# Two constant products in each of TensorE's two later routing waits, in a four-layer transformer kernel on one Trainium2 core

## What is computed

```python
def hierarchical_moe(h, w_rg, b_rg, w_re, b_re, w_gate, w_up, w_down):
    xf = h.reshape(t, d)                                   # t = 256 tokens, d = 1024
    group_logits = xf @ w_rg + b_rg                        # 4 groups
    grp = argmax(group_logits); p_grp = softmax(group_logits)[grp]
    expert_logits = (xf @ w_re + b_re).reshape(t, 4, 8)    # 8 experts in each group
    top_logit, top_local = top_k(expert_logits[grp], 2)    # two experts for each token
    gates = p_grp * softmax(top_logit)
    experts = grp * 8 + top_local
    # the 512 (token, expert) pairs are sorted by expert, cut into blocks, and for each block
    y = (silu(xb @ w_gate[e]) * (xb @ w_up[e])) @ w_down[e]
    # every token adds its two results, each times its gate
```

## Time and profile before

| | |
|---|---|
| median of three runs | 1895.18 us (1894.8 to 1901.27) |
| span of the profiled execution | 1897.5 us |
| the mixture's jobs, first layer | from 857.9 us to about 1250 us of the span |
| the mixture's jobs, second layer | from 1440.3 us to about 1880 us |
| TensorE busy | 1822.5 us, 96% of the span |
| mean granted TensorE clock over the span | 0.987 |
| read from memory | 546.83 MB |

### The profile page before, as it was taken

One profiled execution on the slowest core, in us unless ns is written; L12 is line 12 of the kernel. 1 busy time (PEld: TensorE's weight loads), 2 busy tenths in 40 slices (PEclk: granted clock), 3 DMA queues, 4 the chain that ended last, 5 costly groups with the idle time before them and its releaser, 6 DMA issues.

```text
span 1897.5 us, 27293 instructions
## 1 busy us (share of the span) xinstructions
PE 1822.5 (96%) x10299; PEld 1179.9 (62%) x10299; DVE 861.8 (45%) x1611; ACT 765.6 (40%) x1392; POOL 105.0 (6%) x146
## 2 busy tenths in 40 slices
PE   8999999998999999999999999999999999999997
PEld 6779998886799988974334333335975333433334
DVE  4766656678765566873112111114784111211113
ACT  5554334556543335532333333334542333333333
POOL 3420000112100000010000000000010000000000
PEclk9999999998999999999999999999998999999999
DMA  9545555551355554449999999998557999999995
GB/s 318 201 161 185 193 179 177 166 180 55 110 189 179 181 184 149 162 195 374 419 427 427 427 429 428 429 428 336 186 211 276 411 427 428 427 428 426 428 428 217
DMA packets 130593, 549.40 MB, mean 290 GB/s; under 512 B 8030, under 2 KB 67768, under 8 KB 103480
## 3 DMA queue, kind: packets, MB, share of 16 engines
q1 hardware_dynamic: 127080, 539.53, 72.3%
q0 software_dynamic: 3088, 8.10, 1.3%
q10 hardware_dynamic: 320, 0.34, 0.1%
HBM read 546.83 MB, written 1.11 MB: 289 GB/s over the span
## 4 chain that ended last, share of the span: by engine, by line
PE 75%; DMA 17%; DVE 5%; ACT 1%; POOL 1%; issue 1%; SPq 0%; POOLq 0%; DVEq 0%; ACTq 0%
PE pb L1350 28%; DMA raw<-in_w_expert_down 16%; PE pb L1912 14%; PE pb L1941 11%; PE pb L1645 6%; PE pb L1920 2%; PE pb L1930 2%; PE pb L1479 1%; PE pb L1456 1%; PE pb L1502 1%; PE pb L1579 1%; DVE parts L2104 1%; POOL rms L893 1%; PE pb L1362 1%; PE pb L1858 1%
## 5 line engine op out<-in xcount | busy, mean ns | idle before, releaser
L2104 DVE TENSOR_TENSOR parts<-raw,parts 128x2048 fp32r<-128x2048 f32 (+1 forms) x138 | 307.2, 2232 | 109.3 <-ACT parts L913 106.3
L913 ACT ACTIVATE parts<-raw 128x2048 fp32r<-128x2048 f32 (+1 forms) x138 | 256.6, 1867 | 210.9 <-PE pb L1350 154.4
L1912 PE MATMUL pb<-raw,xw 128*64 128x512 f32 x1360 | 323.9, 608 | 10.9 <-DMA raw<-in_w_expert_gate 10.9
L1350 PE MATMUL pb<-xT,parts 128*128 128x256 f32 (+1 forms) x2712 | 333.3, 283 | 0.0
L1350 PEld LDWEIGHTS pb<-xT,parts 128*128 128x128 f32 (+1 forms) x2712 | 329.2, 191 | 4.7 <-issue 2.9
L2720 DVE TENSOR_TENSOR qk<-qk,pb 128x256 f32<-128x256 f32 x126 | 53.1, 422 | 550.0 <-ACT qk L1205 549.8
L1350 PE MATMUL pb<-parts,xT 128*128 128x512 f32 (+1 forms) x1200 | 273.4, 386 | 2.7 <-DVE xT L2115 1.5
L1350 PEld LDWEIGHTS pb<-parts,xT 128*128 128x128 f32 x1200 | 218.8, 190 | 49.2 <-issue 4.0
L1912 PEld LDWEIGHTS pb<-raw,xw 128*64 128x64 f32 x1360 | 87.5, 138 | 156.4 <-issue 133.3
L1941 PE MATMUL pb<-raw,qk 128*64 128x512 f32 x624 | 142.8, 596 | 20.3 <-DMA raw<-in_w_expert_down 20.2
L1200 ACT ACTIVATE qk<-pb 128x512 f32<-128x512 f32 x126 | 74.9, 595 | 195.4 <-PE pb L1912 195.4
(11 more groups left out here) (338 smaller groups left out, 1692.9 us busy)
## 6 DMA issues: line engine op xcount, KB each, us to landing
raw<-in_w_expert_gate SPq DMA_DIRECT2D x41, 2048.0 KB, 10.0
raw<-in_w_expert_up SPq DMA_DIRECT2D x37, 2048.0 KB, 10.4
raw<-in_w_expert_down SPq DMA_DIRECT2D x35, 2048.0 KB, 10.7
spare<-in_w_expert_down SPq DMA_DIRECT2D x16, 2048.0 KB, 15.1
spare<-in_w_expert_up SPq DMA_DIRECT2D x14, 2048.0 KB, 13.4
raw<-in_w_ffn_gate SPq DMA_DIRECT2D x22, 1024.0 KB, 5.2
raw<-in_w_ffn_up SPq DMA_DIRECT2D x22, 1024.0 KB, 5.1
raw<-in_w_ffn_down SPq DMA_DIRECT2D x22, 1024.0 KB, 4.9
```

What stands on the lines that cost most here:

```text
L913: nc.scalar.activation(parts[:, (SPL0[seg] + k) % SPL, 0, 0:kk * nn], raw[:, place, 0:kk * nn], ACT.Copy).then_inc(hi_done[seg], 1)
L1350: ins = mm(out_ap, b if flip else a, a if flip else b, start=first and n == 0, stop=last and n == 2)
L1912: ins = mm(pb[m][rows, :], xw[:, 4 * hf + k, :], w[:, k, :], start=(hf == 0 and k < 2), stop=(hf == 1 and k >= 2))
L2104: v.tensor_tensor(two[:, 1, :], raw[:, place, 0:kk * nn], two[:, 0, :].bitcast(F32), ALU.subtract)\
```

## The change

Two calls of `spin(2)` are put into TensorE's list in the routing, one behind L1841 and ahead of the wait for the job table's columns, the other behind L1845 and ahead of the wait for the first selection. That is two times four more passes in each of the two layers. Nothing else is changed.

```diff
                 mm(pb[3][0:1, JOBS:2 * JOBS], cst[0:1, C_I512 + W:C_I512 + W + 1], ij, start=True, stop=False).then_inc(pos_ready, 1)
+                spin(2)
                 pe.wait_ge(job_cols, l + 1)
                 ja, jo, jv = jobs_work()
                 mm(pb[3][0:1, JOBS:2 * JOBS], jv, jo, start=False, stop=True)
...
                 def tokens(i, t, k):
                     return xsp[:, i, D * t + P * k:D * t + P * (k + 1)]
 
+                spin(2)
                 for t in range(NT):
                     for i in range(2):
                         if i == 0:
```

## The result

| | median of its runs | ratio to before, 95% interval |
|---|---|---|
| before | 1896.59 us (7 runs, 1894.73 to 1901.27) | |
| changed | 1889.12 us (7 runs) | 0.9949 [0.9934, 0.9963] |
| predicted | 1884.8 us (range 1882.8 to 1891.5) | 0.9945 (1884.8/1895.18) |

The changed kernel is about 0.5% faster. It was timed on three further occasions, each with its own runs of the kernel before beside it: 0.9934, 0.9942 and 0.9945, medians 1885.71, 1887.46 and 1887.52 us. By the medians the gain was 7.5, 11.5, 9.5 and 9.8 us, and their plain quotients are 0.9961, 0.9940, 0.9950 and 0.9948, so 0.4 to 0.6%.

The account below looks back on a forecast made before the run. It took DMA to set each layer's end, with holes where loads wait for a half-clocked TensorE. 4.8 + 4.8 + 0.8 = 10.4 us off 1895.2 gave 1884.8 us, range 1882.8 to 1891.5 us.

Parts of the forecast that it names:

- the 3.3 us ahead of the fall: Routing stretch before the clock drops: TensorE busy 1.17 us, 2.9 us with both calls, like a stretch that kept its clock.
- The cost of the two calls: Routing waits: first call delays the table's product 0.05 us (bound 0.2), second delays the gather 0 (bound 0.1).
- The gain on TensorE: Gather and job 0 at full clock in place of half: L1874 starts 5.0 us earlier a layer.
- The short stop ahead of the last eight: In the gather, the last 8 of 32 products wait for VectorE's low parts until 853.66 us, costing nothing.
- DMA passes it on: In the expert jobs, weight loads follow the earlier TensorE, so 4.8 us a layer reaches the layer's end.
- rival 1: In the expert jobs, DMA returns only its idle time, not all its shortfall: 4.9 us, 1890.3 us; chance 0.28.
- DMA's holes: First layer's jobs, 860 to 890 us: DMA at 292 and 383 GB/s, 5.3 us lost, which an earlier TensorE fills.
- The dip at 930 us: First layer's jobs: DMA at 381 GB/s, 1.1 us lost; the load waits for TensorE and shifts with it.
- The 0.15 us that were taken off for DMA: Deduction a layer for what DMA can't follow around 930 us, estimated as a seventh of 1.1 us.
- The third term: Second layer's spin(8), starting earlier, may meet less half clock: 0.8 us taken, bounds 0 and 1.6 us.
- The forecast's own range: Whole kernel: 1883 to 1887 us if the forecast's mechanism holds, which had chance 0.56.
- The rule on idle gaps: Skill page's rule: only clearly longer TensorE gaps cost the clock, so filling these waits changes nothing, 1895.2 us.

Follow-up runs that it names:

- e2: Only the first `spin(2)`, ahead of the wait for the job table's columns, added to the kernel before: 1898.28 us, ratio 1.0001.
- e4: `spin(1)` in place of `spin(2)` at both places of the change: 1897.03 us, ratio 1.0000 to the kernel before.
- e7: `spin(4)` at both places, added to the kernel before: 1890.92 us, ratio 0.9959.
- e8: Changed kernel with its spin(8) split, four products ahead of the row products and four behind: 1889.69 us, ratio 0.9953 to the kernel before.
- e9: Changed kernel with the spin(8) split into two spin(4), plus spin(3) in the wait this opened: 1885.50 us, ratio 0.9940 to the kernel before.
- e3: Only the second `spin(2)`, ahead of the selection's wait, added to the kernel before: 1898.03 us, ratio 1.0003.
- e1: The changed kernel again, no edit, against the kernel before: 1885.71 us, ratio 0.9934.
- e5: The changed kernel once more, no edit, against the kernel before on another occasion: 1887.46 us, ratio 0.9942.
- e10: The changed kernel on a further occasion, no edit, against the kernel before: 1887.52 us, ratio 0.9945.
- e6: `spin(4)` at the second place alone, ahead of the selection's wait, added to the kernel before: 1893.76 us, ratio 0.9979.

## Why the prediction was right, point by point

**The clock is the cause, and both waits are needed.** Right as far as the change goes: the traces of its three repetitions hold 1.00 from L1824 through job 0 in both layers. The prediction argued from the busy time of the 3.3 us ahead of the fall. e2 to e4 show how weak that is as a measure: the clock fell in a stretch busy for 2.97 of 3.35 us. What they support is narrower: in these runs four products of 128x256 in the two waits kept the clock, two didn't, and four in the second wait alone did so in one layer of two. Why the clock falls where it does stays open; that its fall is what cost the time is shown, since the gather and job 0 hold the same products in all these kernels and took 14.0 to 16.2 us with the fall and 10.9 to 11.0 us without.

**The cost of the two calls.** Predicted 0.05 us and 0 of bounds 0.2 and 0.1; measured 0 for both, to 0.01 us. The margin is thin, as e7 shows: the next two products cost 0.84 us.

**The gain on TensorE, 5.0 us a layer.** Measured 4.73 us, in both layers. Two pieces are missing. Job 0 starts 3.88 us behind the gather and not 3.71. The products of the gather came 0.111 us apart and not 0.107, half of their spacing at half clock, so that VectorE's scaling, which needs the 28th, began 3.40 us behind the gather's start and not 3.2. The short stop ahead of the last eight did not show: L2573 ends at 855.92 us, and the 25th product starts at 856.00 us, 0.11 us behind the 24th like all others. And job 0 takes 7.02 us and not 6.85, up to L1876's start. Here the prediction's own figures don't agree: 5.3 us for 23.8 records is 0.223 us each, or 7.1 us for all 32, and not 0.213. The records do come 0.213 us apart, but the first and the last step take longer.

**DMA passes it on.** Right, and rival 1 is out: TensorE's 4.73 us are all there at the second layer's logits (553.21 us between before, and 553.08, 553.03 and 553.12 us in the three traces of the change), and DMA's holes are filled. It stayed full behind them and made up the hole, since it had lost more than TensorE gained. The dip at 930 us stayed, as predicted, because the load there waits for TensorE. The 0.15 us that were taken off for DMA were not needed. The time alone would not have shown this: 1889.12 us is nearer to rival 1's 1890.3 than to the forecast's 1884.8, and it is the traces that rule rival 1 out.

**The third term, 0.8 us.** The times can't tell it, and the traces speak for more than was taken. These are the lengths of the half clock, in us, at the places where the traces differ, beside e7's in the jobs. The spin(8) of e8 and e9 is split, so their columns for it mean the same stretch of the routing.

| trace | about 93 us | spin(8), first layer | gather, first layer | spin(8), second layer | gather, second layer |
|---|---|---|---|---|---|
| before, e2 | 3.4 | 3.4 | 10.2 | 6.8 | 10.2 |
| e3 | 3.4 | 3.4 | 10.2 | 6.8 | 13.6 |
| e4 | none | 6.8 | 6.8 | 6.8 | 10.2 |
| the change (e1, e5, e10), e7 | 6.8 | 6.8 | none | 3.4 | none |
| e6 | 6.8 | 6.8 | none | 3.4 | 10.2 |
| e8 | 3.4 | none | 13.6 | none | 13.6 |
| e9 | none | none | none | none | none |

The prediction said that the second layer's spin(8) may meet less half clock, because all is earlier there. In all five traces with the spin(8) whole in which the first layer's gather kept its clock it met 3.4 us, and in the four in which the clock fell there it met 6.8. That is 1.65 us, just beyond the bound of 1.6, where 0.8 was taken. The first layer's 6.8 us in place of 3.4 cannot be the change's, since they lie ahead of the first new product, and the column of 93 us differs already. In the spans they hide the gain in the second layer. These are single executions, so how often either happens is open. The runs of the change range over 6 us, those with a mean granted clock of 0.994 at 1884.1 to 1885.5 us and those with 0.991 at 1888.6 to 1890.5. All three profiled ones are of the second kind, so that no trace shows where the others had less half clock; it moves a run's time by as much as a layer's gain.

**The sum.** Twice 4.73 is 9.5 us, and 11.1 with the 1.65 us of the second layer, against 10.4. The four medians give 7.5 to 11.5 us, 9.6 on average, so they don't decide between these. From the 1896.6 to 1897.3 us of the kernel before on the four occasions 9.5 us lead to 1887.1 to 1887.8 us; measured were 1885.7 to 1889.1. Of the 4.3 us between the forecast and 1889.12, 1.4 us are the median of three runs that it started from, 1895.18 us, and 2.9 us the gain of 7.5 in place of 10.4. The forecast's own range, 1883 to 1887 us, holds one of the four medians; two lie 0.5 us above it and one 2.1 us. The wider range holds all four, but 1889.12 us lies in the part of it that was there for rival 1, which did not happen. So the mechanism was right, and that the range held this median was partly luck. The line of 0.5%, 9.5 us, is just where the gain lies, so that faster or the same was an even matter, and 0.44 to 0.53 was a fair price for it.

**The rule on idle gaps.** The Trainium skill, page "TensorE: Matmul & The Clock Gate", section "Why this matters for your kernels", warns of long idle gaps between bursts. The runs don't agree with it as a sufficient rule: in e4 the gaps were 0.38 and 0.50 us, and the clock fell. And filling waits of 1.01 and 1.12 us, which by that rule would change nothing, gave 4.73 us a layer.

## What to carry to other kernels

Look for stretches at 0.50 in the clock column and read what TensorE did ahead of them. Here it was short products of few rows or columns, with waits of about 1 us for another engine, and the bill was paid by the big products behind. Filler cost nothing here where its array time (0.85 us) was less than the wait (1.01 and 1.12 us), and it had to be enough: one call alone or one product in each wait gave nothing, four products in one wait gave a part, and twice the total cost 1.3 us a layer. When DMA bounds the stage behind, ask whether it had holes that were TensorE's. Here they were larger than the gain (6.4 us against 4.73), and the gain passed through whole; what a gain beyond them would do was not tried. And before a stretch of two traces is put down to a change, see whether it lies behind the first changed instruction.

## What was not expected of the hardware

- Half clock came in lengths of 3.4, 6.8, 10.2 and 13.6 us in the traces, and the same routing code met 3.4 us in one layer and 6.8 in the other. Such a difference moved the work behind it by 1.65 us.
- In the kernel before the clock did not come back during the gather's products of 128x128, back to back at half clock for over 6 us, but in job 0's products of 128x512; in the earlier wait it came back during the constants of 128x256, after 3.4 or 6.8 us. Whether the kind of product or the moment decides is not shown.
- A move of work to the front can cost the clock: in e8's trace L1824 came earlier, and behind the new wait of 0.95 us the clock fell for 13.6 us.
